# A four-layer hybrid decoder step on one core: the gated pieces at the end of the recurrent layers, in another order

## What is computed

```
o, s = gla_recurrence(q, k, v, logf, s0)          # per head: o is (tokens, 256), 4 heads
o = rmsnorm(o, g_on)                               # over the 256 values of a head
dp = (o * silu(g)) @ w_out                         # g = h @ w_in[:, gate columns]
y = y + dp                                         # layer 3: then the final rmsnorm
```

## Time and profile before

| | |
|---|---|
| time, median of 3 runs | 1141.79 us (1141.3 to 1143.9) |
| the profiled execution: its own time | 1145.38 us |
| its span, first to last instruction | 1143.7 us |
| instructions | 25413 |
| PE busy | 1109.3 us (97%) |
| DVE, ACT, POOL busy | 666.0 us (58%), 485.6 us (42%), 379.7 us (33%) |
| mean granted TensorE clock | 0.992 of full speed |

### The profile page before, as it was taken

The page is one execution under the profiler, slowest core; times in us unless marked ns, Lnnn a source line. Parts: engine busy times, 40 slices in busy tenths (PEclk is TensorE's granted clock), DMA queues, the critical chain, the costliest instruction groups (busy, mean ns, idle before and its releaser), DMA issues. The chain is left out here.

```text
span 1143.7 us, 25413 instructions
## 1 busy us (share of the span) xinstructions
PE 1109.3 (97%) x10509; PEld 966.5 (85%) x10509; DVE 666.0 (58%) x1214; ACT 485.6 (42%) x955; POOL 379.7 (33%) x321
## 2 busy tenths in 40 slices
PE   7999999999999999999999999999999999999996
PEld 6889988899758988889955599999999889988875
DVE  6462354864899879777444656596445272245533
ACT  6541467543443312222354554322453352376632
POOL 4534313234313413114300044354345245311240
PEclk9999999999999999999999999999999999999998
DMA  5335252233314787884779942233220315335112
GB/s 168 105 111 166 74 182 96 93 83 100 111 59 144 238 273 238 284 307 153 258 292 409 379 117 84 68 108 109 97 80 3 111 58 183 100 130 178 38 56 79
DMA packets 125722, 169.31 MB, mean 148 GB/s; under 512 B 20441, under 2 KB 89689, under 8 KB 125600
## 3 DMA queue, kind: packets, MB, share of 16 engines
q1 hardware_dynamic: 113401, 152.85, 40.1%
q10 hardware_dynamic: 12206, 14.85, 3.6%
HBM read 151.22 MB, written 16.81 MB: 147 GB/s over the span
## 5 line engine op out<-in xcount | busy, mean ns | idle before, releaser
L755 POOL TENSOR_TENSOR w_lo<-raw,w_hi 128x512 fp32r<-128x512 f32 (+2 forms) x267 | 357.3, 1368 | 688.3 <-ACT w_hi L1550 688.3
L791 PE MATMUL psum<-h_hi,w_hi 128*128 128x272 f32 (+1 forms) x1488 | 433.3, 291 | 4.7 <-DVE h_lo L2528 2.8
L793 PE MATMUL psum<-h_hi,w_lo 128*128 128x272 f32 (+1 forms) x1488 | 430.6, 289 | 0.0
L792 PE MATMUL psum<-h_lo,w_hi 128*128 128x272 f32 (+1 forms) x1488 | 428.0, 288 | 0.0
L791 PEld LDWEIGHTS psum<-h_hi,w_hi 128*128 128x128 f32 (+1 forms) x1488 | 279.3, 188 | 15.5 <-issue 8.2
L792 PEld LDWEIGHTS psum<-h_lo,w_hi 128*128 128x128 f32 (+1 forms) x1488 | 279.6, 188 | 0.1
L793 PEld LDWEIGHTS psum<-h_hi,w_lo 128*128 128x128 f32 (+1 forms) x1488 | 278.9, 187 | 0.0
L1550 ACT ACTIVATE w_hi<-raw 128x1024 fp32r<-128x1024 f32 (+1 forms) x137 | 135.6, 1035 | 124.0 <-PE psum L793 85.1
L791 PE MATMUL psum<-w_hi,h_hi 128*128 128x512 f32 (+2 forms) x416 | 152.5, 367 | 3.0 <-issue 2.0
L793 PE MATMUL psum<-w_hi,h_lo 128*128 128x512 f32 (+2 forms) x416 | 148.0, 356 | 0.2 <-issue 0.2
L792 PE MATMUL psum<-w_lo,h_hi 128*128 128x512 f32 (+2 forms) x416 | 148.2, 356 | 0.0
(11 more groups left out here) (334 smaller groups left out, 1384.5 us busy)
## 6 DMA issues: line engine op xcount, KB each, us to landing
smp_keys<-in_cache_k_dram SPq DMA_DIRECT2D x128, 256.0 KB, 4.6
raw<-in_gla_w_in_dram SPq DMA_DIRECT2D x23, 1024.0 KB, 5.3
raw<-in_dsa_w_in_dram SPq DMA_DIRECT2D x17, 1024.0 KB, 5.4
spare<-in_cache_v_dram SPq DMA_DIRECT2D x34, 512.0 KB, 7.9
raw<-in_cache_v_dram SPq DMA_DIRECT2D x30, 512.0 KB, 8.7
gla_s_in<-in_state_gla_dram SPq DMA_DIRECT2D x16, 512.0 KB, 4.9
raw<-in_gla_w_out_dram SPq DMA_DIRECT2D x8, 1024.0 KB, 5.0
out_dram<-gla_s_in ACTq DMA_DIRECT2D x16, 512.0 KB, 3.0
```

Of the source, the lines that this page charges most:

```text
L755: pool.tensor_tensor(copies(key, pair_view(w_lo, key)[:, k]), raw_copies(key, k), copies(key, pair_view(w_hi, key)[:, k].bitcast(F32)), AL ...
L791: pe.matmul(out, lh, rh, start=start, stop=False)
L792: pe.matmul(out, lh, rl, start=False, stop=False)
L793: return pe.matmul(out, ll, rh, start=False, stop=stop)
```

## The change

Three orders change, in both GLA layers, since they share the code. On PE, piece 2 is turned together with pieces 0 and 1, ahead of `gate_job(15)`, rather than behind it. On DVE, the decode result is copied out of PSUM ahead of the copy for tile 3, piece 2 is gated straight behind pieces 0 and 1, its remainder is taken straight behind `gate_part(15)`. On ACT, pieces 0 and 1 are rounded ahead of the squares of tile 3; the squares of the decode tile follow at once; then comes piece 2, now ahead of the silu of block 7 and behind a new explicit wait for the end of `gate_job(15)`; and the table load and the root of tile 3 and decode tile now stand ahead of the second half of the weight rounding, not behind it. No arithmetic is added or taken away.

```diff
--- before.py
+++ after.py
@@ -1016,7 +1016,6 @@
                                            start=False, stop=k == KT - 1)
                     mm.then_inc(*sig("proj", ("Y", n, SMP)))
 
-                out_transposes(L, 2, 0)
                 rows_job(0, 0, 0, True)
                 out_transposes(L, 0, 1)
                 out_transposes(L, 1, 1)
@@ -1214,14 +1213,14 @@
                         for n in (4 * t + 3, 4 * t + 4, 4 * t + 5):
                             gate_job(n)
                     else:
-                        out_transposes(L, 0, 0)
-                        out_transposes(L, 1, 0)
+                        for x in range(3):
+                            out_transposes(L, x, 0)
                         gate_job(15)
 
                 if L == LAST:
                     out_rows(L)
                     return
-                for t, half in OUT_PIECES[2:6]:
+                for t, half in OUT_PIECES[3:6]:
                     out_transposes(L, t, half)
 
                 def last_rows():
@@ -1820,8 +1819,7 @@
                     sequence(2 * t + 1)
                     if t < NP_T - 1:
                         decay(2 * t + 2)
-                    squares(t)
-                    if t < NP_T - 1:
+                        squares(t)
                         decay(2 * t + 3)
                         gate_block(2 * t + 1)
                         act.preload_act_table_set(EXP_LN)
@@ -1833,16 +1831,18 @@
 
                 branch_hi(0)
                 branch_hi(1)
+                squares(NP_T - 1)
+                squares(SMP)
+                act.wait_ge(*on("proj", (L, "g", KT - 1), 1))
+                branch_hi(2)
                 gate(L, gate_g, KT - 1, ("gate_dve", (L, "g", KT - 1), 1))
-                branch_hi(2)
                 branch_hi(3)
                 split_hi(pair_of[(L, "out", 1)], (0,))
                 branch_hi(4)
                 branch_hi(5)
+                act.preload_act_table_set(EXP_LN)
+                root(slice(12, 17), SMP)
                 split_hi(pair_of[(L, "out", 1)], (1,))
-                act.preload_act_table_set(EXP_LN)
-                squares(SMP)
-                root(slice(12, 17), SMP)
                 act.wait_ge(*on("s_now", L, NCH))
                 act.dma_start(gla_state_prompt[j, 0].rearrange("h k v -> k h v"),
                               s_now[:, 0, :].rearrange("p (h v) -> p h v", h=GH)).then_inc(*sig("stores_gla", L, n=16))
@@ -2498,6 +2498,8 @@
                     if t < NP_T - 1:
                         add_state(2 * t + 2)
                         mask(t + 1)
+                    else:
+                        out_rows(SMP)
                     out_rows(t)
                     if t == NP_T - 1:
                         break
@@ -2535,20 +2537,18 @@
                         dve.wait_ge(*on("h_lo", (L, "out"), *OUT_PIECES[i - 4]))
                     gated(*OUT_PIECES[i], tmp_og[:, i % 4])
 
-                piece(0)
-                piece(1)
+                for i in range(3):
+                    piece(i)
                 low(0)
                 low(1)
                 gate_part(15)
-                piece(2)
+                low(2)
                 piece(3)
-                low(2)
                 piece(4)
                 low(3)
                 piece(5)
                 low(4)
                 low(5)
-                out_rows(SMP)
                 root(slice(12, 17), SMP)
                 normalise(3)
                 normalise(SMP)
```

## The result

The changed kernel took 1145.61 us in the median of six runs (1143.0 to 1146.64); the kernel before took 1141.01 in the six runs beside it (1139.72 to 1143.9). The ratio is 1.003, with a 95% interval from 1.0017 to 1.0043. That is slower by 3.4 us, more than the noise of this kernel; the medians lie 4.6 apart and the means 4.1, so the size is known to about 1.5 us only. A second series of the unaltered changed kernel gave 1145.43 (11 runs) and 1.0028 [1.0012, 1.0045].

The account below looks back on a forecast made before the run. PE, busy 97% of the span, was taken as the bound. Layer 0 path +0.47, clock +1.5 and layer 3 path +0.52 make +2.5 on the median 1141.79: 1144.3 us, range 1141.0 to 1146.3.

Parts of the forecast that it names:

- The two path terms: Later turning of tile 3 without the clock: +0.47 us in layer 0 (late silu), +0.52 in layer 3 (late weight half).
- First wait of layer 0: PE's wait for the remainder of piece 2 shrinks by 0.77 us; PE starts at 214.79 rather than 215.56.
- Silu 7: Layer 0, on ACT: silu stands behind rounding 2 and starts 0.48 us later, with everything after it following.
- Second wait and remainders: Layer 0: last two remainders take turns with POOL; PE waits 2.6 us in one piece and goes on 0.47 later.
- The clock in layer 0: PE's clock falls to the lower level behind the 2.6 us wait: +1.5 us, range 0 to 1.7.
- Layer 3: Weight half 1.84 us later, PE waits 1.2 and 0.75 for POOL, `normalise` alternates with POOL; tile 3 turned 0.52 later.
- The clock in layer 3: Waits of 1.2 and 0.75 us with one k between may lower the clock: 0 to +1.5, taken as 0.
- Rival A: No fall of the clock in layer 0: +1.0, 1142.8 us; chance 0.25.
- rival B: The clock falls in both layers: +4.0, 1145.8 us; chance 0.12.
- Rival C: Layer 0: remainders 4 and 5 run before POOL, clock stays: -1.3 +0.52, 1141.0 us; chance 0.08.
- Rival D: Late weight half does no harm in layer 3; layer 0's 1.3 and layer 3's 1.37 gained: -2.7, 1139.1 us; chance 0.05.

Follow-up runs that it names:

- Kernel 5: Changed kernel, both layers, with silu 7 ahead of rounding 2, gating 3 ahead of remainder 2, decode tile's squares between roundings 4 and 5: 1142.88 us, ratio 1.0000.
- kernel 1: The whole change made in layer 0 only, layer 3 in the old order: 1143.66 us, ratio 1.0011.
- kernel 3: Changed kernel with the second weight half put back ahead of table load and root, in both layers: 1144.36 us, ratio 1.0017.
- kernel 10: The changed kernel unaltered, run again for more executions: 1145.43 us (11 runs), ratio 1.0028.
- kernel 4: Changed kernel with layer 0's first weight half moved behind rounding 5, so POOL is idle during the last two remainders: 1143.40 us, ratio 1.0008.
- kernel 2: The whole change made in layer 3 only, layer 0 in the old order: 1142.97 us, ratio 1.0007.
- kernel 8: Layer 0 as before the change; layer 3 as in kernel 7, with load and root right behind rounding 2: 1140.44 us, ratio 0.9977.
- kernel 7: Changed kernel with, in layer 0, silu first and weight halves behind the last rounding; in layer 3, load and root right behind rounding 2: 1141.39 us, ratio 0.9992.
- kernel 9: Layer 0 in the order of kernel 5 (silu first), layer 3 in that of kernel 8 (early root): 1140.43 us, ratio 0.9990.
- kernel 6: Changed kernel with matmuls nobody reads filling PE's waits, 18 in layer 0, four and one in layer 3: 1144.42 us, ratio 1.0011.

## Why the prediction was right, and which term was too small

The forecast was 1144.3, in the range 1141.0 to 1146.3; the time was 1145.61. On the ratio it was +2.5 against a measured +3.4 (interval 1.9 to 4.9), and +3.2 in the second series (1.4 to 5.1). The two path terms were right in mechanism and size. That the sum came so near is in part luck: no profile of the changed kernel shows the case that it describes, a fall in layer 0 and none in layer 3. The first profile had it the other way round, so the fall that was put at nothing stood in for the one that was counted. Going through its steps:

- **First wait of layer 0.** Forecast: PE goes on at 214.79, that is 6.74 behind the first turning; measured 212.62 - 205.83 = 6.79. The wait was forecast as 0.69 (1.46 less 0.77) and is 0.95, since PE came to it 0.21 sooner than I had it (5.84 behind the first turning; before, 215.56 - 1.46 - 208.05 = 6.05).
- **Silu 7.** Forecast 0.48 later, measured 0.51. Kernel 5 shows that it is the cause: with the silu earlier, the waits of before return.
- **Second wait and remainders.** Forecast 2.6 in one piece, measured 2.56, and 2.54 to 2.57 in kernels 1, 3 and 10. The remainders took turns with POOL again (1.37 and 1.75), and kernel 4 shows that it is POOL. The cost in layer 0 without the clock was forecast as +0.47 and is 17.23 - 16.73 = +0.50.
- **The clock in layer 0.** Forecast +1.5; one fall costs 1.50. The sign that I had named for it, a stretch near 0.5 behind the second wait, was missing in the first profile. It does not fall each time: behind this wait it did in three profiles of four (kernels 1, 3 and 10, not in the first profile of the changed kernel). The mean of this term is then rather 1.1, an estimate from four executions.
- **Layer 3.** With 1072.14 - 1071.25 = 0.89 added, the changed kernel's rows read on the forecast's scale. POOL's start: forecast 1088.74, measured 1088.76. `normalise`: forecast 1088.41 to 1092.29, measured 1088.44 to 1092.15. PE's third product: 1090.1 and 1090.11; its fourth: 1091.60 and 1091.53. The waits are 1.07 and 0.46 rather than 1.2 and 0.75, as PE came to them a little later. The cost without the clock was forecast as +0.52 and is +0.49 (kernel 4). `normalise` and POOL alternate, as taken.
- **The clock in layer 3.** Here is the term that was mis-sized. I wrote "0 to +1.5, and I take 0". In the five profiles with these two waits, not filled, it fell in three (the changed kernel, kernels 2 and 10) and not in two (kernels 4 and 5). A window of 4.00 us at 0.60 is 1.6 us of work not done, and to the end of the span the profiles with a fall are 1.6 longer (73.6 and 71.95), so this term is rather +1.0 in the mean, again an estimate, from five executions. Behind the one wait of 1.37 of before, or 1.17 in kernel 3, it fell in none. I had read the trace of before as if only a long wait could be followed by a fall; its own falls behind the sixteen small matmuls, at 50.9 and 914.4 us with 0.53 of wait ahead, would have spoken against taking 0 for two waits close together.

Added up: 0.50 + 0.49 + 1.1 + 1.0 is 3.1. The measured +3.4 and +3.2 of the ratios agree with it, the means (+4.1 and +3.5) within their uncertainty of nearly 1. The clock term can be had in a second way, from every run of the second series rather than from the profiled ones: the mean granted clock was 0.9939 over the 11 runs of the changed kernel and 0.9961 over the 22 of before on the same chip; 0.0022 of 1143 us is 2.5. Of the 3.5 that leaves 1.0 for the waits, where the traces have 0.99. So close an agreement is chance, given that uncertainty; that the clock is a large part of it is not.

Rival A (no fall in layer 0) and rival B (falls in both layers) are thus not alternatives between which the chip chose. They are both what single executions of one program do: the first profile is A's layer 0 with B's layer 3, the last one is B. Together with the falls elsewhere that is the likely reason why its runs spread from 1140.84 to 1150.95: over the 17 of them time and mean granted clock have a correlation of -0.92. I had given 0.44 to a change that is slower by over 0.2%, and 0.50 to none that can be told. Rival C, remainders slipping past POOL, did not happen. Kernel 4 made it happen, and `normalise` took the loss. Rival D, no harm from the late weight half, fell with the 1.07 us wait; its other half, the gain of 1.37 from an early root, is real, and kernel 8, which moves the weight halves as well, collects it by putting load and root into idle time rather than ahead of something that PE waits for.

The Trainium skill's rule that I set against the trace (TensorE: Matmul & The Clock Gate, section HAM oscillation), by which only longer gaps should matter, is not borne out here: falls stood behind 2.54 and 2.57 us, behind 2.03, behind 1.06 with 0.46 close to it, and in the stage of small matmuls behind 0.53. The one on shared ports (SBUF — State Buffer, section Who interferes with whom) is: 0.68 became 1.37 and 1.75 for the remainders, and 1.67 became 3.71 for `normalise`.

What stays open is what decides whether the clock falls behind a given wait. The same waits at the same distance did both. No run here varied anything else alone, so the frequencies above are counts from a few profiles and not rules.

## What to carry to other kernels

Two waits of about 1.4 us on TensorE with 3.3 us of work between them cost no more than themselves here; shifting idle time from the first into the second made one of 2.56, and with it, in three of four profiles, a clock fall worth 1.5 us, three times the 0.5 by which the path had grown. Two waits with a single product between them, 1.07 and 0.46, were not safe: three falls in five. When an instruction is moved forward on an engine, look first for what it pushes back, and whether the whole chain hangs on that; here a square of 0.4 and a rounding ahead of the silu, and a table load ahead of a weight half that had 0.12 of slack. Put such work into a stretch where the engine is idle with nothing late behind it, even if that is several microseconds earlier than needed.

## What the runs showed of the hardware

- Four `SCALAR_TENSOR_TENSOR` of 128x256 with two operands in SBUF take 1.67 us alone, 3.60 beside two subtractions of POOL that begin 0.19 ahead of them, 3.71 beside two that begin 0.32 behind their start. The POOL instructions went from 2.54 to 2.72 and 2.71. Instructions on 128x5 went from 0.17 to 0.68, 0.69 and 0.79 when POOL was in one, and ended within 0.03 us of it (kernels 4, 3 and before); in layer 3 of kernel 8 three of them in a row took 1.25, 1.21 and 1.21. An instruction of 128x5 thus lost as much as one of 128x256 (1.49 rather than 0.48 in the changed kernel). So for these instructions beside POOL their number counted, not their size.
- Falls of the clock behind waits that stood alone, counted over all twelve profiles and all layers: none behind any wait from 0.90 to 1.89 us, among them one of 1.77 or 1.78 in layer 1 of every profile; five behind the nine from 1.98 to 2.24 (fallen in before, the changed kernel, kernels 2, 7 and 9; not fallen behind 2.05 in kernel 4, 2.19 in kernel 7 and 2.04 in each of kernels 9 and 10); three in four behind 2.54 to 2.57; and one with a wait of 3.39 in layer 1 of kernel 6. Kernel 6, with the idle time filled by matmuls that nobody reads, had none in the two filled places.
- Falls also stood behind sixteen small matmuls with 0.53 us of wait, in 12 of 24 cases. Length of wait alone does not tell where the clock falls.
- Over 92 runs of the kernel before, the time falls by 0.9 us for each 0.001 of mean granted clock (0.989 to 0.998, 1148.96 to 1139.86, correlation -0.87). A large part of the spread between executions of one program is therefore how often its clock fell.
